# Three held gate jobs instead of two: 24 pieces of projection work inside block 0's attention A

## The reference, cut to what matters

```python
h = rmsnorm(x, norm1_g)
proj = h @ w_in          # A: q, k, v | B: q, latent | indexer: q, k, w | gate_a (1024), gate_b (1024)
o_a = mixer_a(...)       # window attention, 8 heads, T5 bias and sinks
o_b = mixer_b(...)       # top 256 keys of an indexer's scores, then attention over them
merged = sigmoid(gate_a) * (o_a @ w_branch_a) + sigmoid(gate_b) * (o_b @ w_branch_b)
x = x + merged @ w_out
x = x + (silu(h2 @ w_ffn_gate) * (h2 @ w_ffn_up)) @ w_ffn_down     # h2 = rmsnorm(x, norm2_g)
return rmsnorm(x, norm_f_g)
```

## Time and profile before

| | |
|---|---|
| median of 3 runs | 3209.31 us (3209.04 to 3215.2) |
| the profiled execution's own time | 3214.48 us |
| its span, from the first to the last instruction | 3212.7 us |
| TensorE busy | 3158.1 us, 98% |
| VectorE, ScalarE, GpSimd busy | 1822.4, 1419.3, 2031.7 us |
| mean granted clock of TensorE | 0.997 |

### The profile page before, as it was taken

The page is one execution under the profiler, slowest core; times in us unless marked ns, Lnnn a source line. Parts: engine busy times, 40 slices in busy tenths (PEclk is TensorE's granted clock), DMA queues, the critical chain, the costliest instruction groups (busy, mean ns, idle before and its releaser), DMA issues.

```text
span 3212.7 us, 43895 instructions
## 1 busy us (share of the span) xinstructions
PE 3158.1 (98%) x15612; PEld 2653.2 (83%) x15612; DVE 1822.4 (57%) x3706; ACT 1419.3 (44%) x2589; POOL 2031.7 (63%) x2201
## 2 busy tenths in 40 slices
PE   8999999999999999999999999999999999999998
PEld 6888888878888888888888888988888799888887
DVE  4236546537565546557666766967867679521111
ACT  3324435435463534337454534836655368320001
POOL 5666666665556666764666676376666922666676
PEclk9999999999999999999999999999999999999999
DMA  5765455355615333332533333163333410533332
GB/s 143 200 172 170 119 157 154 102 157 164 205 35 182 103 112 105 108 125 69 197 104 110 100 108 133 26 238 101 98 102 112 165 33 20 176 93 97 94 104 99
DMA packets 464201, 392.59 MB, mean 122 GB/s; under 512 B 29264, under 2 KB 394064, under 8 KB 463344
## 3 DMA queue, kind: packets, MB, share of 16 engines
q1 hardware_dynamic: 442544, 345.56, 35.7%
q10 hardware_dynamic: 21440, 44.22, 3.7%
HBM read 323.76 MB, written 62.81 MB: 120 GB/s over the span
## 4 chain that ended last, share of the span: by engine, by line
PE 89%; DVE 4%; ACT 3%; POOL 2%; issue 2%; DMA 0%; ACTq 0%; SPq 0%; DVEq 0%; POOLq 0%
PE BANK L1049 20%; PE BANK L1050 20%; PE BANK L1051 20%; PE LP L1049 3%; PE LP L1051 3%; PE LP L1050 3%; PE BANK L1322 3%; PE BANK L1347 2%; PE LP L1166 2%; PE LP L1302 2%; PE LP L1165 2%; PE LP L1303 2%; PE BANK L1349 2%; POOL WLO L986 1%; PE BANK L1358 1%
## 5 line engine op out<-in xcount | busy, mean ns | idle before, releaser
L986 POOL TENSOR_TENSOR WLO<-WRAW,WHI 128x512 fp32r<-128x512 f32 x912 | 1217.5, 1335 | 76.1
L984 POOL TENSOR_SCALAR WHI<-WRAW 128x512 fp32r<-128x512 f32 x912 | 632.1, 693 | 767.0 <-PE BANK L1051 617.1
L1049 PE MATMUL BANK<-H2hi,WHI 128*128 128x512 f32 x1376 | 539.5, 392 | 1.3 <-POOL WLO L986 1.3
L1050 PE MATMUL BANK<-H2lo,WHI 128*128 128x512 f32 x1376 | 536.7, 390 | 0.0
L1051 PE MATMUL BANK<-H2hi,WLO 128*128 128x512 f32 x1376 | 536.4, 390 | 0.0
L1049 PE MATMUL BANK<-HThi,WHI 128*128 128x512 f32 (+1 forms) x1024 | 405.9, 396 | 0.6 <-ACT GS L1833 0.3
L1050 PE MATMUL BANK<-HTlo,WHI 128*128 128x512 f32 (+1 forms) x1024 | 400.1, 391 | 0.0
L1051 PE MATMUL BANK<-HThi,WLO 128*128 128x512 f32 (+1 forms) x1024 | 399.8, 390 | 0.0
L1743 ACT ACTIVATE MASK<-SCD,THR 128x896 bf16<-128x896 f32 (+5 forms) x186 | 281.9, 1516 | 199.0 <-DVE THR L2096 170.7
L1051 PEld LDWEIGHTS BANK<-H2hi,WLO 128*128 128x128 f32 x1376 | 258.7, 188 | 54.6
L1049 PEld LDWEIGHTS BANK<-H2hi,WHI 128*128 128x128 f32 x1376 | 258.9, 188 | 54.1 <-issue 1.3
(11 more groups left out here) (312 smaller groups left out, 6461.4 us busy)
## 6 DMA issues: line engine op xcount, KB each, us to landing
WRAW<-in_w_in SPq DMA_DIRECT2D x124, 512.0 KB, 4.3
WRAW<-in_w_ffn_gate SPq DMA_DIRECT2D x88, 512.0 KB, 3.8
WRAW<-in_w_ffn_up SPq DMA_DIRECT2D x88, 512.0 KB, 3.8
WRAW<-in_w_ffn_down SPq DMA_DIRECT2D x88, 512.0 KB, 3.6
qsp<-QS SPq DMA_DIRECT2D x32, 512.0 KB, 5.7
WRAW<-in_w_out SPq DMA_DIRECT2D x32, 512.0 KB, 4.6
gates<-GS ACTq DMA_DIRECT2D x62, 256.0 KB, 2.7
GL<-gates ACTq DMA_DIRECT2D x48, 256.0 KB, 4.5
```

The lines of the kernel that those rows point to most:

```text
L984: nc.gpsimd.tensor_scalar(hi, raw, 1.0, 1.0, ALU.mult, ALU.mult).then_inc(w_hi, 1)
L986: nc.gpsimd.tensor_tensor(lo, raw, hi.bitcast(f32), ALU.subtract).then_inc(w_split, 1)
L1049: nc.tensor.matmul(dst, whi, mhi, start=first, stop=False)
L1050: nc.tensor.matmul(dst, whi, mlo, start=False, stop=False)
```

## The change

`HELD` becomes the last three gates of block 3, m = 13, 14 and 15. The held steps become -9 to -2 (gate 13), 0 to 7 (gate 14) and 9 to 16 (gate 15); they were -9 to -3 and -2, 0, 2 and so on to 14. So `trans` gets its third bank at step 18 instead of 16, and ScalarE's `keep_gate` comes at its steps -1, 8 and 17 instead of -1 and 15. GpSimd leaves out the split of the last gate in its order of jobs and does its two halves at steps -1 and 1 of block 0's attention. `gates_before` counts the gate writes that ScalarE has to see on either semaphore.

```diff
-        HELD = range(2 * KT - 2, 2 * KT)
+        HELD = range(2 * KT - 3, 2 * KT)
...
-        HELD_STEPS = list(range(-9, -2)) + list(range(-2, 15, 2))
+        HELD_STEPS = list(range(-9, -1)) + list(range(0, 8)) + list(range(9, 17))
         AFTER = 10
+
+        def gates_before(m, r):
+
+            return (NB - 1) * KT + (m + 1 - r) // 2
...
                             add_sink(u)
                             lower_near(u)
+                            if u in (2, 3):
+                                split_half(first_job - 1, u - 2)
...
-            def split(i, between=None):
+            def split_half(i, a):
                 key, src = JOBS[i]
                 width = min(src.shape[2], P)
-                pool.wait_ge(w_in_sem[i % 2], 16 * (i // 2 + 1))
-                if i >= 2:
-                    pool.wait_ge(bank_full, n(bank_full, JOBS[i - 2][0]))
+                if a == 0:
+                    pool.wait_ge(w_in_sem[i % 2], 16 * (i // 2 + 1))
+                    if i >= 2:
+                        pool.wait_ge(bank_full, n(bank_full, JOBS[i - 2][0]))
...
+                nc.gpsimd.tensor_scalar(hi, raw, 1.0, 1.0, ALU.mult, ALU.mult).then_inc(w_hi, 1)
+                pool.wait_ge(w_hi, 2 * i + a + 1)
+                nc.gpsimd.tensor_tensor(lo, raw, hi.bitcast(f32), ALU.subtract).then_inc(w_split, 1)
+
+            def split(i, between=None):
                 for a in range(2):
                     if a and between is not None:
                         between()
...
+                    split_half(i, a)
...
+                if key == ("gate", NB - 1, HELD[-1]):
+                    continue
                 if key[0] != "br" or key[2] > 1:
                     split(i, (lambda: near_norm(key[1] + 1, scaled[0])) if scaled else None)
...
                         for r in range(2):
-                            act.wait_ge(gate_out[r], 16 * (NB * KT - 1))
+                            act.wait_ge(gate_out[r], 16 * gates_before(HELD[0], r))
...
                     act.wait_ge(bank_full, n(bank_full, ("gate", NB - 1, m)))
-                    act.wait_ge(gate_out[m % 2], 16 * (NB * KT - 1))
+                    act.wait_ge(gate_out[m % 2], 16 * gates_before(m, m % 2))
                     if m != HELD[0]:
-                        act.wait_ge(gate_out[(m - 1) % 2], 16 * NB * KT)
+                        act.wait_ge(gate_out[(m - 1) % 2], 16 * gates_before(m, (m - 1) % 2))
```

More of the change, by code:

```diff
@@ L971, in attend @@
                         split_low(i - end_at(b, "b", free) - 2)
-            def split(i, between=None):
+            def split_half(i, a):
                 key, src = JOBS[i]
                 width = min(src.shape[2], P)
-                pool.wait_ge(w_in_sem[i % 2], 16 * (i // 2 + 1))
-                if i >= 2:
-                    pool.wait_ge(bank_full, n(bank_full, JOBS[i - 2][0]))
+                if a == 0:
+                    pool.wait_ge(w_in_sem[i % 2], 16 * (i // 2 + 1))
+                    if i >= 2:
+                        pool.wait_ge(bank_full, n(bank_full, JOBS[i - 2][0]))
+                raw, hi, lo = (w[i % 2][:, :, 0:width].rearrange("p (e c) w -> p e c w", c=2)[:, :, a, :] if key[0] == "br"
+                               else w[i % 2][:, a * SLOTS // 2:(a + 1) * SLOTS // 2, 0:width] for w in (WRAW, WHI, WLO))
+                nc.gpsimd.tensor_scalar(hi, raw, 1.0, 1.0, ALU.mult, ALU.mult).then_inc(w_hi, 1)
+                pool.wait_ge(w_hi, 2 * i + a + 1)
+                nc.gpsimd.tensor_tensor(lo, raw, hi.bitcast(f32), ALU.subtract).then_inc(w_split, 1)
+            def split(i, between=None):
                 for a in range(2):
```

## The result

| | before | after |
|---|---|---|
| median | 3210.89 us (3207.47 to 3215.2, 20 runs) | 3214.21 us (3211.34 to 3222.25, 20 runs) |
| ratio | 1 | 1.0013, 95% interval 1.0007 to 1.0019 |
| profiled execution, its span | 3214.48, 3212.7 | 3216.16, 3214.4 |

The changed kernel is slower by 4.2 us (0.0013 of 3210.9; the interval gives 2.2 to 6.1; the means differ by 4.1, the medians by 3.3). I had forecast +0.2. The change is within 0.2%, but its direction is clear of the noise, and I had forecast none.

What follows compares the result with a forecast made beforehand. TensorE, busy 98% of the 3212.7 us span, was taken as the bound. Terms -5.8 + 3.6 + 2.4 gave +0.2 us, predicting 3209.5 us, between 3207.5 and 3212 with chance 0.54; within 0.2% had 0.84.

Steps and rivals of the forecast that it cites:

- Term 3: Shifted banks make the FFN's first gates wait for later row tiles: +2.4 us, bounds 1.5 and 5.
- 1.0 us a block: Cost of `first_gate` starting 2.15 us later after `wo` in blocks 0 and 2; bounds 0.7 and 2.15.
- 0.1 each, four times: 0.4: Cost in us of the next gate waiting for row tile j=3 after the first two `fd`.
- rival 1: Clock stays up in block 0's attention, wait at step 1 shrinks to 1.85: -3.6 us, 3205.9; chance 0.22.
- Rival 3: New bubble at ScalarE's step 8 drops the clock from 886.20 to 904.00: +7.6 us, 3217.1; chance 0.05.
- Term 2: Block 0's attention takes eight more held-gate pieces: +3.6 us, bounds nothing and 7.8.
- the bubble of 1.68 at step 8: TensorE's fold at step 8 waits because the second `keep_gate` delays PThi and PTlo: forecast 1.4 us.
- Term 1: One gate job leaves the projections, so block 0's attention starts earlier, its wait on bank 3 gone: -5.8 us.
- The wait of 1.85 at step 1: TensorE's 2.53 us wait for VectorE's maxima partly filled by a free piece, leaving 1.85 us.
- Rival 4: The banks don't bite because VectorE's adds are in time: -2.4 us, 3207.1; chance 0.07.
- rival 5: Splits in block 0's attention delay VectorE's maxima of steps -1 to 2 by up to 3.8 us: 3213.3; chance 0.04.
- rival 2: All pieces in block 0's attention hidden and both clock falls gone: near 3202.1 us, faster by 0.22%; chance 0.08.

Runs made afterwards that it cites:

- e2: The kernel before with the ring `bank` turned on three places ahead of block 0's branches, so it takes the changed kernel's banks; ratio 1.0009.
- e4: The kernel before with only the last gate's split moved into GpSimd's steps -1 and 1 of block 0's attention; ratio 0.9998.
- e12: The kernel before, unchanged, traced a second time; block 0's attention, first logits to last fold but one, took 87.59 us.
- e1: The changed kernel with the ring `bank` turned on one place ahead of block 0's branches, so it takes the banks of before; ratio 0.9998.
- e9: The changed kernel, banks of before, held-gate copy behind PThi and XV, second gate's pieces doubled at steps 0 and 1, third gate at 7 to 14; ratio 0.9982.
- e11: The kernel before, two held gates, held-gate copy behind PThi and XV, second gate's pieces at steps 0, 0, 1, 1, 2, 3, 4, 5; ratio 0.9992.

## Why the prediction was wrong

**Term 3 (the banks) was too small, and this is shown.** The cause was right, with its place: `first_gate` starts at 1043.61, that is 2.15 later than before once everything ahead is taken out (0.68 against -1.47), the shift that I had worked out. What failed is the step "1.0 us a block", with its bounds of 0.7 and 2.15. It priced a wait of 2.6 us on TensorE as time without work alone. As that price it was about right: block 2 of after, without a fall, cost 0.84, to about 1 us. But behind the other waits the clock fell, and 18 matmuls took 3.40 us for 2.25. With a fall a `first_gate` cost 2.35 to 2.40 (block 0 of after, both blocks of e2), above my upper bound. The smaller part, "0.1 each, four times: 0.4", measured 0.19 each, and 1.0 to 1.3 with some 0.17 that each of the two blocks loses between `first_gate` and the first `fd`. Together 4.5 to 5.7 where I had 2.4. I had taken account of exactly this, a fall behind a wait, in rivals 1 and 3, and not here.

**Term 2 (the attention) was too small against an ordinary execution.** Forecast +3.6; against the profiled execution of before it is +3.44, near to it, but by errors that cancel. Up to the fold of step 8 I had +2.5; that fold now stands 29.88 us behind the first logits. In before it is 31.75, in e2 29.72. So the pieces up to there are nearly hidden, which is what rival 1 said; the clock stayed up in this execution. From there to step 18 I had won back 1.5 us of low clock. It was not won: the bubble of 1.68 at step 8 (I had 1.4) brought 4.70 us at 0.64, and that at step 16 (1.96; I had 2.4) brought 8.40 us at 0.59. Against the lengths of e2, e4 and e12 the changed order (94.17, 93.98, 92.69) takes 5.9 us more, against all four of before 5.1: nearly the 5.44 that left the projections. The working also has a slip: its parts for TensorE at step 18 (1.6, 1.36, 1.0, 1.4, less 1.5) add up to 3.9 and not to 4.5.

**The base was at fault too.** "The profile lies 5.2 above it, which I don't explain, and I carry the difference over." Part of it was the fall of 9.80 us behind step 1, a stretch on which I had built the costs of steps 1 to 8 and half of rival 1. It isn't a property of the order. Eleven executions wait 1.48 us or more at this place (e4 in two parts), and behind it the clock fell in five. Five of the eleven have the order of before, and of these it fell in two, for 3.5 and 9.8 us. The length of the wait doesn't decide it: it was 2.53 in those two and in two where the clock stayed up.

**What held.** Term 1: 5.13 at the first logits and 5.59 at the first held piece (-5.37 less 0.22), the GS wait gone, for 5.8. The wait of 1.85 at step 1, three copies at the forecast places, the bubble near step 8 (though in after only 0.61 of its 1.68 are for PTlo, and 1.07 for ON; in e1 it is 1.23 and 0.45), the split at no cost, `first_gate` of blocks 0 and 2 waiting for the addition to X and that of blocks 1 and 3 not. Rival 4 falls by e1 and e2, rival 5 by e4, rival 2 by the two low stretches of the trace. Rival 3 came in small: the new bubble did drop the clock behind step 8, for 4.70 us and not 17.80, though it stayed under the 1.75 that I had set.

**The sum again:** -5.1 (projections), +5.1 to +5.9 (attention), +4.5 to +5.7 (banks) gives +4.5 to +6.5. Measured are +4.2 (2.2 to 6.1). e1, the same without the banks, gives 0 to +0.8 so; measured is -0.6, give or take 1.4. The sum is at the upper side of both and I don't settle the rest: the share of executions in which the clock falls at step 1 isn't known for either kernel.

## What to carry to other kernels

Taking one user out of a ring of buffers moves every later user to another buffer. Count the takes modulo the ring's length at each place where a second ring shares the banks: here that side effect cost more than the edit's own mechanism, and one line took it back. Price a new wait of TensorE twice, once as the wait and once as a possible low stretch behind it (here the first came to about 0.8 us and the second to 1.5, for waits of 2.6 to 3.05), and fill it with work if there is any. The kernel with the third gate that was 4 us slower than before was 7 us faster when the pieces stood in the waits and the copies behind what others wait for. And if a profile lies above the median, look for what that execution had that others may not before you build on it; a second look at the same kernel would have shown it.

## What I had not expected of the hardware

- Whether the clock falls behind a wait is not settled by the wait. Waits of 2.53 us at one place in one order: it fell behind two (0.50 for 9.8 us, 0.55 for 3.5) and stayed at 1.00 behind two. Waits of 1.82: it fell behind three of five. Waits of 0.44 there (e9 to e11): none of three. At `first_gate`, 2.6 to 3.05 us: three of four. For OTA near 2250, 2.71 to 2.75 us, in all fourteen traces: nine of fourteen.
- Executions differ already at 95.76 us, where no edit has touched an instruction yet, by up to 3.4 us over the fourteen traces (after is 0.22 later than before, e2 3.19 earlier). The spread arises in the first 20 us and hardly grows from there up to 600. I didn't look for the cause; it is as large as the effects studied here, and is a reason to compare stretches and not spans.
